# Delta mixer in 128-token tiles, its head pairs run between the input blocks; RWKV matrices alternating between heads

## The reference

```python
def mixer_c(h, w_in, conv_w, A_log, dt_bias, norm_w, w_out):
    z = h @ w_in
    qkv = jax.nn.silu(causal_dwconv(z[..., :3 * W], conv_w))
    ...
    q = l2norm(qkv[..., :W].reshape(b, s, DN_HEADS, DN_HEAD_DIM)) * (DN_HEAD_DIM ** -0.5)
    k = l2norm(qkv[..., W:2 * W].reshape(b, s, DN_HEADS, DN_HEAD_DIM))
    o = gated_delta_rule_chunked(q, k, v, g, beta)
    o = rmsnorm(o, norm_w) * jax.nn.silu(gate.astype(F32))
    return o.reshape(b, s, W).astype(h.dtype) @ w_out
```

```python
    def step(state, inp):
        v_new = u_c - jnp.einsum('bhck,bhkv->bhcv', w_c, state)
        o = jnp.einsum('bhck,bhkv->bhcv', qd_c, state) + jnp.einsum('bhij,bhjv->bhiv', at_c, v_new)
        state = state * cd_c[..., None, None] + jnp.einsum('bhck,bhcv->bhkv', kd_c, v_new)
        return state, o
```

## Time and profile before

| what | value |
|---|---|
| median of the runs | 2514.31 us |
| profiled execution | 2503.3 us, of which the span of instructions is 2501.5 us |
| TensorE matmul busy | 2377.8 us (95%) |
| VectorE, ScalarE, GpSimd busy | 1236.1, 802.5, 253.2 us |
| mean granted TensorE clock | 0.94 of full speed |
| mixer C, from its first to its last matmul | 1564.9 to 2124.5 us |

### The profile page before, as it was taken

The page is one execution under the profiler, slowest core; times in us unless marked ns, Lnnn a source line. Parts: engine busy times, 40 slices in busy tenths (PEclk is TensorE's granted clock), DMA queues, the critical chain, the costliest instruction groups (busy, mean ns, idle before and its releaser), DMA issues.

```text
span 2501.5 us, 29427 instructions
## 1 busy us (share of the span) xinstructions
PE 2377.8 (95%) x11460; PEld 1957.0 (78%) x11460; DVE 1236.1 (49%) x1528; ACT 802.5 (32%) x1053; POOL 253.2 (10%) x180
## 2 busy tenths in 40 slices
PE   6999999979988999999999999999888988999997
PEld 5888887748975888888888888877777876888886
DVE  5444445586524644443444443885665117544423
ACT  4232223452213433222323222356423124323221
POOL 1000010005500100001000011000453001000011
PEclk9999999989956999999999999999989558999999
DMA  4333323200010233332223332321000001333331
GB/s 144 98 95 99 113 83 97 76 1 1 1 35 26 93 100 92 104 104 94 85 93 100 102 104 80 96 90 51 1 1 35 1 17 59 93 96 97 111 97 52
DMA packets 48256, 182.40 MB, mean 73 GB/s; under 512 B 6320, under 2 KB 6576, under 8 KB 48176
## 3 DMA queue, kind: packets, MB, share of 16 engines
q1 hardware_dynamic: 48176, 181.29, 23.0%
HBM read 179.17 MB, written 2.10 MB: 72 GB/s over the span
## 4 chain that ended last, share of the span: by engine, by line
PE 73%; DVE 4%; ACT 2%; issue 1%; DVEq 0%; ACTq 0%
PE bank L437 18%; PE bank L439 18%; PE bank L438 18%; PE bank L500 3%; PE bank L511 3%; PE bank L822 1%; PE bank L821 1%; PE bank L607 1%; PE bank L842 1%; PE bank L833 1%; PE bank L636 1%; PE bank L851 1%; PE bank L641 1%; PE bank L514 1%; PE bank L763 1%
## 5 line engine op out<-in xcount | busy, mean ns | idle before, releaser
L437 PE MATMUL bank<-H,WS 128*128 128x512 f32 x1840 | 726.8, 395 | 26.8 <-DVE WS L1262 16.9
L438 PE MATMUL bank<-H,WS 128*128 128x512 f32 x1840 | 718.5, 390 | 0.0
L439 PE MATMUL bank<-H,WS 128*128 128x512 f32 x1840 | 718.2, 390 | 0.0
L878 ACT ACTIVATE WS<-RAW 128x1024 fp32r<-128x1024 f32 (+1 forms) x310 | 349.0, 1126 | 1082.0 <-PE bank L439 1061.0
L1262 DVE TENSOR_TENSOR WS<-RAW,WS 128x1024 fp32r<-128x1024 f32 (+1 forms) x310 | 404.6, 1306 | 252.1 <-ACT WS L878 252.0
L437 PEld LDWEIGHTS bank<-H,WS 128*128 128x128 f32 x1840 | 346.8, 188 | 108.8 <-DVE WS L1262 14.4
L438 PEld LDWEIGHTS bank<-H,WS 128*128 128x128 f32 x1840 | 346.9, 189 | 75.2 <-issue 3.8
L439 PEld LDWEIGHTS bank<-H,WS 128*128 128x128 f32 x1840 | 347.0, 189 | 72.4
L437 PE MATMUL bank<-A,WS 128*128 128x512 f32 x704 | 273.9, 389 | 0.0
L438 PE MATMUL bank<-A,WS 128*128 128x512 f32 x704 | 273.9, 389 | 0.0
L439 PE MATMUL bank<-A,WS 128*128 128x512 f32 x704 | 273.9, 389 | 0.0
(11 more groups left out here) (306 smaller groups left out, 2330.0 us busy)
## 6 DMA issues: line engine op xcount, KB each, us to landing
RAW<-in_w_gate SPq DMA_DIRECT2D x88, 512.0 KB, 3.5
RAW<-in_w_up SPq DMA_DIRECT2D x88, 512.0 KB, 3.5
RAW<-in_w_down SPq DMA_DIRECT2D x64, 704.0 KB, 4.0
RAW<-in_c_in SPq DMA_DIRECT2D x32, 512.0 KB, 3.6
RAW<-in_ab_in SPq DMA_DIRECT2D x22, 512.0 KB, 3.6
RAW<-in_ab_out SPq DMA_DIRECT2D x8, 512.0 KB, 4.4
RAW<-in_c_out SPq DMA_DIRECT2D x8, 512.0 KB, 4.1
X<-in_x SPq DMA_DIRECT2D x4, 512.0 KB, 7.2
```

The source lines that it names most:

```text
L437: pe.matmul(bank[:, :], WS[:, 0, s, cols], src[0][:, r, :], start=first and j == 0, stop=False)
L438: pe.matmul(bank[:, :], WS[:, 0, s, cols], src[1][:, r, :], start=False, stop=False)
L439: mm = pe.matmul(bank[:, :], WS[:, 1, s, cols], src[0][:, r, :], start=False, stop=last and j == len(rows) - 1)
L878: act.activation(WS[:, 0, c % SPLIT, 0:cols], RAW[:, c % RING, 0:cols], ACT.Copy).then_inc(hi_ready, 1)
```

## The change

Three things are changed.

**Mixer C works in tiles of 128 tokens.** The inverse is built for 128 tokens: after the five levels (blocks of 32, then 64) two more small products per tile join the two halves (`c_u21_mm`, `c_xt64_mm`). The solve gives u and w side by side (256 columns). The transitions are then computed in advance: for each tile a 128 x 128 matrix MT (decay times identity minus w-transposed times decayed keys) and an addition N, so that the scan is only state := MT x state + N, two steps per head (the first state is zero, the last is not needed). The outputs are one product per tile with the tile's own values plus one with the state (3 of 4 tiles). L2 norms are not applied to keys and queries; they enter as per-token factors, summed by matmuls with one column.

**Head pairs run between input blocks.** The input blocks come in the order key, query, value of a pair of heads, pair after pair, then the gates (`C_ORDER`). A unit is cut into 4 slots of 6 matmuls (`slot`). 8 units run alone; then each pair's `core(p)` runs with 24 slots between its steps. VectorE and ScalarE do the convolution, activation and splitting of a unit in `piece()`, called at the matching places. SiLU is now x(1 + tanh(x/2))/2, the first convolution tap is made by ScalarE. GpSimd multiplies token factors into RHS and KDT (6 more instructions per pair) beside the 12 masked TM. The output projection starts with the rows of heads 0 to 5.

**RWKV matrices alternate.** `matrices(b)` issues head 2b and head 2b + 1 in turn, and VectorE masks them in that order.

The core of the diff (semaphore names, allocations and the small scalar steps are left out):

```diff
+    mats += [s <= t, np.where(s <= t, 0.0, -30000.0)]
...
-                                mm = pe.matmul(BANK[4 * s + k][:, c], left[rows, b, c], right[rows, b, c],
-                                               start=True, stop=True)
-                            mm.then_inc(mat_mm[s], 1)
+                                for s in range(2):
+                                    rows = slice(s * CHUNK, (s + 1) * CHUNK)
+                                    mm = pe.matmul(BANK[4 * s + k][:, c], left[rows, b, c], right[rows, b, c],
+                                                   start=True, stop=True)
+                                    if j == TT - 1:
+                                        mm.then_inc(mat_mm[s], 1)
...
+                    def slot():
+                        t, k = divmod(next(dense), 4)
+                        if k == 0 and t >= 2:
+                            pe.wait_ge(*c_z(t - 1))
+                        unit(BANK[t % 2], u0 + t, 0, H_PARTS, (2 * k, 2 * k + 1), k == 0, k == 3, norm=n if t == 0 else None,
...
+                        for s in range(2):
+                            b0, b1, b2 = banks(s)
+                            pe.wait_ge(*c_tt(2 * p + s + 1))
+                            pe.wait_ge(*c_silu(6 * p + 2 + s + 1))
+                            for c in cols:
+                                mm = pe.matmul(b1[:, c], K[s][:, c], QQ[s][:, c], start=True, stop=True)
+                            mm.then_inc(c_qk_mm.sem, 1)
+                        slot()
...
+                        slot()
+                        if p:
+                            heads_back(p - 1)
+                        for s in range(2):
+                            b0, b1, b2 = banks(s)
...
+                        for l in range(5):
+                            for s in range(2):
...
+                                for j, c in enumerate(cols):
+                                    mm = pe.matmul(b0[:, c], CS[s]["TM"][:, j, :], CS[s]["XX"][:, j, :], start=True, stop=True)
+                                mm.then_inc(c_u_mm.sem, 1)
+                            slot()
+                            for s in range(2):
+                                b0, b1, b2 = banks(s)
+                                pe.wait_ge(*c_iu(10 * p + 2 * l + s + 1))
...
+                                for j, c in enumerate(cols):
+                                    mm = pe.matmul(b2[:, c], CS[s]["XT"][:, j, :], CS[s]["IU"][:, j, :], start=True, stop=True)
+                                mm.then_inc(c_xx_mm.sem, 1)
...
+                            slot()
...
+                        for s in range(2):
+                            b0, b1, b2 = banks(s)
+                            pe.wait_ge(*c_u21(2 * p + s + 1))
+                            pe.wait_ge(*c_xt32(2 * p + s + 1))
+                            for j, c in enumerate(halves):
+                                mm = pe.matmul(b2[lo, c], CS[s]["U21"][hi, j, :], CS[s]["XT"][hi, j, hi], start=True, stop=True)
+                            mm.then_inc(c_xt64_mm.sem, 1)
...
+                        for s in range(2):
...
+                            for j in range(TT):
+                                if j == 2 and p < 3:
+                                    pe.wait_ge(*c_kn(p + 2))
+                                mm = pe.matmul((b0, b1)[j // 2][:, j % 2 * 2 * P:(j % 2 + 1) * 2 * P], CS[s]["XT"][:, j, :],
+                                               CS[s]["RHS"][:, j, :], start=True, stop=True)
+                                if j % 2:
+                                    mm.then_inc(c_solve_mm.sem, 1)
+                        slot()
...
+                            w = CS[s]["UW"][:, :, P:2 * P]
+                            for j in (1, 2):
+                                mm = pe.matmul(b2[:, cols[j - 1]], w[:, j, :], CS[s]["KDT"][:, j, :], start=True, stop=True)
+                            mm.then_inc(c_mt_mm.sem, 1)
+                            for j in range(3):
+                                mm = pe.matmul(b0[:, cols[j]], CS[s]["KDT"][:, j, :], CS[s]["UW"][:, j, 0:P], start=True, stop=True)
+                            mm.then_inc(c_n_mm.sem, 1)
+                            for j in (1, 2, 3):
+                                mm = pe.matmul(b1[:, cols[j - 1]], w[:, j, :], CS[s]["ATT"][:, j, :], start=True, stop=True)
+                            mm.then_inc(c_qw_mm.sem, 1)
+                        slot()
+                        for k in range(2):
+                            for s in range(2):
+                                b0, b1, b2 = banks(s)
+                                pe.wait_ge(*c_mt(2 * p + s + 1))
+                                if k == 0:
+                                    pe.wait_ge(*c_n(2 * p + s + 1))
+                                else:
+                                    pe.wait_ge(*c_state(4 * p + s + 1))
+                                pe.matmul(b2[:, cols[2 + k]], CS[s]["MT"][:, k, :], CS[s]["NS"][:, k, :],
+                                          start=True, stop=True).then_inc(c_scan_mm.sem, 1)
+                            slot()
+                        for s in range(2):
+                            b0, b1, b2 = banks(s)
+                            pe.wait_ge(*c_state(4 * p + 2 + s + 1))
+                            pe.wait_ge(*c_qw(2 * p + s + 1))
...
+                    for m in range(2):
+                        mixed_rows(m, range(6))
+                    heads_back(3)
+                    for m in range(2):
+                        mixed_rows(m, (6, 7))
+                    for m in range(2, KB):
+                        mixed_rows(m, range(KB))
...
+                                act.wait_ge(*(c_ktr_mm, c_out_mm, c_vtr_mm)[kind](2 * (p - 2) + s + 1))
+                            act.activation(c_place(t)[:, :], PAD[:, t % 2, 3:3 + SEQ], ACT.Copy,
+                                           scale=par("dn_conv_w", 72 + C_ORDER[t])).then_inc(c_tap.sem, 1)
+                        u = t - 1
+                        if k == 2 and 0 <= u < C_BLOCKS:
+                            act.wait_ge(*(c_conv if u < 24 else c_z)(u + 1))
+                            if u:
+                                act.wait_ge(*c_silu(u))
...
+                            for s in range(2):
+                                h = 2 * p + s
+                                if l == 1:
+                                    pool.wait_ge(*c_ktok(2 * p + s + 1))
+                                    pool.wait_ge(*c_decays(1))
+                                    pool.tensor_tensor(CS[s]["RHS"][:, :, P:2 * P], CS[s]["KDT"][:, :, :], token_cols(EG[:, :, h]),
+                                                       ALU.mult).then_inc(c_ke.sem, 1)
...
+                                pool.wait_ge(*c_u_mm(10 * p + 2 * (l - 1) + s + 1))
+                                pool.tensor_tensor(CS[s]["TM"][:, :, :], CS[s]["TT"][:, :, :], tiles(con(f"pair{2 << l}")),
+                                                   ALU.mult).then_inc(c_tm.sem, 1)
                 squares(norm_of[phase] + 1)
...
+                        for k, (name, mask) in enumerate((("TT", "strict"), ("TKM", "strict"), ("MKM", "upper"))):
+                            for s in range(2):
+                                dst = {"TT": INV[s]["TT"], "TKM": TKM[s], "MKM": MKM[s]}[name]
...
+                        if k == 0 and 0 <= t < C_BLOCKS:
+                            vec.wait_ge(unit_done, u0 + t + 1)
+                            vec.tensor_tensor(pad[:, 3:3 + SEQ] if t < 24 else GATE_C[:, t % 4, :], BANK[t % 2][:, :], RSTD[:, :],
+                                              ALU.mult).then_inc(c_z.sem, 1)
...
+                        if k == 1 and 1 <= t < C_BLOCKS:
+                            split_lo(u0 + t + 2, 0)
+                        if k == 2 and dst is not None:
+                            vec.wait_ge(*c_z(t + 1))
+                            vec.wait_ge(*c_tap(t + 1))
+                            for r in (2, 1):
+                                step.wait()
+                                step.inc(vec.scalar_tensor_tensor(dst[:, :], pad[:, r:r + SEQ], par("dn_conv_w", 24 * r + C_ORDER[t]),
+                                                                  dst[:, :], ALU.mult, ALU.add))
+                        if k == 2 and 0 <= t - 26 < 6:
...
+                                                     ALU.mult, ALU.add).then_inc(c_conv.sem, 1)
+                        u = t - 1
+                        if k == 3 and 0 <= u < C_BLOCKS:
+                            x_ = KQV[u // 6 % 2][u % 6 // 2][u % 2][:, :] if u < 24 else GATE_C[:, u % 4, :]
+                            vec.wait_ge(*c_tanh(u + 1))
+                            vec.scalar_tensor_tensor(x_, TANH[:, :], 1.0, x_, ALU.add, ALU.mult).then_inc(c_silu.sem, 1)
...
+                        vec.wait_ge(*c_rn(p + 1))
+                        for s in range(2):
```

(27 more changed lines are left out.)

934 lines of the change are left out of this document (542 added, 392 removed).

## The result

| | before | after |
| --- | --- | --- |
| median of the runs | 2514.3 us (4 runs, 2514.1 to 2514.8) | 2382.2 us (4 runs, 2381.7 to 2383.0) |
| span of the profiled execution, mean clock | 2501.5 us, 0.940 | 2379.9 us, 0.968 |
| up to the first matmul of mixer C | 1564.9 us | 1558.2 us |
| mixer C, first matmul to the first of the next layer | 559.6 us | 444.6 us |
| from there to the end | 377.0 us | 377.1 us |

Ratio 0.9475, 95% interval 0.9458 to 0.9491. In later comparisons the executions of the kernel before fell into two groups, 2502 to 2506 us and 2514 to 2516 us; the four runs above were all in the upper one, its profiled execution in the lower. Span against span the change is worth 121.6 us: 115.0 in C and 6.6 ahead of it. The profiled execution's own time after was 2381.7.

A forecast was written before the change was run, and what follows sets the result against it. TensorE, busy 95% of the span, was taken as the bound. C's work 410.7 plus waits 48.5 gave 459.2 instead of 559.6 (100.4 less); with AB's 8.8, 2514.3 - 109.2 = 2405 us, range 2358 to 2445.

The forecast's parts named there:

- TensorE's work in C: Mixer C: four pairs' products 180.0 us, 40 units 218.4, plus tail columns, layer norm, small ones and first norms: 410.7 us.
- Clock 1.00 throughout: Mixer C: full clock assumed, because dense slots stand between products of the kind that run at 1.00 alone.
- rival C: Pairs of mixer C: small products and waits bring 1.2 GHz; 2595 us at 60% half clock; chance of slower than before 0.03.
- Decay matrix: Mixer C's pairs: attention products wait for TT, made by VectorE and ScalarE; 2.5 us per pair, 10 us.
- outputs back: Mixer C: transposes back wait for the previous pair's scaled outputs, late on VectorE; 4 us in three pairs, 12 us.
- first units: Mixer C's first 8 units: VectorE needs 5.0 of each 5.46 us, plus small dependent steps with table loads; 3 us wait.
- end: Mixer C after the last pair: some 16 us of dependent steps beside 8.2 of TensorE work; 5.5 us with one split wait.
- VectorE and GpSimd: Mixer C's levels: VectorE instructions with both operands in SBUF wait out GpSimd's, delaying IU; 4.5 us per pair, 18 us.
- Mixer AB: Alternating heads: a pair's matrices near 3.5 us, inversion 8.9 us behind their start; 2.2 us less per pair, 8.8 us.
- rival A: Mixer C: TensorE hardly waits because GpSimd and VectorE run ahead within a pair; 2365 us, chance 0.26.
- B: Mixer C's pairs: VectorE becomes the bound, 98 us per pair instead of 89; 2441 us, chance 0.22.
- D: Mixer AB: alternating heads does nothing, or products still run one by one; 2414 us, chance included in the forecast's 0.46.

The follow-up runs named there:

- Experiment 10: Kernel before, with 156 useless 128 x 128 x 128 float32 products put between the small products of mixer C's scan: 2507.3 us, ratio 0.9997.
- experiments 7 and 8: GpSimd's factors cut to 4 columns after the first pair, OTOK on ScalarE: 2373.7 us; changed kernel with the factors on ScalarE: 2375.8 us.

## Why the prediction was right, and where it was off

- **TensorE's work in C.** Forecast 410.7 us. Measured: 444.6 less 23.3 of waits less some 11 at half clock (0.03 x 340 + 0.04 x 48.6 = 12.1 by the windows, a part of it idle) gives 410. The sum of products by their pace came out within a microsecond, in part by luck, since misses of some us cancel. Two terms were too large, by about 6 us together: the 64 x 64 products with their switches (9.4 instead of 13.6 us: 0.13 us each at full clock instead of 0.16, 0.1 per switch into them instead of 0.2 per switch either way), and single-column norms (0.21 to 0.24 us instead of 0.25). Against them a slot took 1.38 instead of 1.37 (2 us in all), a transpose term was 1 us too small, and some 2 us are not assigned. The prediction had the price of a switch from the earlier trace rows, an idle 0.33 us; that row is one of the weight loads, beside which the matmuls went on. The same idle stands at each switch into the 64 x 64 products of the changed kernel, and the first of them starts 0.33 us behind the last dense matmul, where 0.23 is usual:

```profile
1764.73 0.40 PE L508 MATMUL bank<-H,WS 128*128 128x512 f32 x1
1765.06 1.14 PE L944 MATMUL bank<-c_XT,c_U 64*64 64x64 f32 x16
1765.06 1.00 PEld L944 LDWEIGHTS bank<-c_XT,c_U 64*64 64x64 f32 x16 [0.36 <-issue]
```

The Trainium skill (TensorEngine Tiling (Array Packing), Key Properties) says that a change of tiling mode drains TensorE. The idle weight loads agree with it; the price here was about 0.1 us.
- **Clock 1.00 throughout.** Nearly: 0.97 in the pairs. Experiment 10 shows that the old 0.58 came with the small products and goes when large ones stand between them. What I left out is what follows an idle stretch: in C there were six stretches of 3 to 6 us at 0.50, four behind waits of 2.6 to 4.2 us and two behind single-column norms and 64 x 64 products with hardly any idle. They cost the 11 us, and the latter two are rival C's mechanism in small.
- **Waits.** Forecast 48.5, measured 23.3. Decay matrix 10 against 4.0, outputs back 12 against 10.3, first units 3 against 0.4, end 5.5 against 4.0. The mis-sized term is "VectorE and GpSimd", 18 us: in the levels TensorE waited for IU not once but for the 4.2 us at the first pair's first level, which come from that pair's opening. The mechanism (an instruction with two SBUF operands waits out GpSimd's) is real, and experiments 7 and 8 price GpSimd's factors at 6.4 to 8.5 us (3.6 and 7.2 by the traces of C). But it acts where VectorE has no slack; in the levels it had some (busy 25.1 of the 30.0 us from 1726 to 1756, second pair). The Trainium skill's rule on the shared port (SBUF — State Buffer, SBUF: two separate sides) agrees with these rows (1.78 against 0.77, 3.44 against 1.28); it says who waits, not whether anybody waits for the one that does.
- **A pair.** Forecast 86 to 90, measured 85.3. Of the distance, the levels' 4.5 us were not there, and 1.6 us or more of half clock were.
- **Mixer AB.** The alternation works (3.7 against 3.5 us forecast), and the inversion starts 8.55 us behind (8.9 forecast). The new wait of 0.89 us for both heads' last copy, in front of each next pair's matrices, I had missed: with it a pair of AB takes 29.8 instead of 31.3 us, and the sum is 6.6 instead of 8.8.
- **The sum.** C 115.0 against 100.4, AB 6.6 against 8.8: span against span 121.6 against 109.2. C's 14.6 are about 25 us of waits forecast that were not there, less 11 at half clock that were not forecast.
- **The step from the profile to the median.** I carried the 11 us between before's profiled execution and its median over to the changed kernel. That failed: they were the distance of two groups of executions, and after has its profiled execution (2381.7) at its median. Without this step the forecast would have been 2394, 12 us above the measurement; with it, 2405, 23 above. The measured time is inside the range given, but in what rival A had for its own, although its mechanism holds only in part.
- **Rivals.** A (TensorE hardly waits) was near in the levels and wrong in the openings. B (VectorE's bound) is right for 25 us of a pair, wrong for the other 60; the 58 us of VectorE per pair that both worked with held (58.05 busy in the second pair). C's mechanism cost a few us. D is out.

What stays open: what decides whether an execution of before falls into the lower or the upper group. Of the 132 us between the medians, 121.6 are what the traces show, and the changed kernel against the lower group's 2503.5 gives 121.3; the other 11 are the group that the first runs of before fell into.

## What to carry to other kernels

Price a redesign by counting products and multiplying by their pace in the trace: that part came out within 1 us of 411, with errors of up to 6 us that cancelled. Compare span with span before a distance between a profile and a median is carried over to another kernel. A wait at a tile can be the lateness of the whole engine that makes it; before moving the tile, list what stands in that engine's queue ahead of it, and what the next tile in line would wait. And where the granted clock is low though TensorE is never idle, look at the shapes: added work in large products cost nothing at all there.

## What the runs showed of the hardware

- The scan of 64-wide float32 products ran at 1.2 GHz while busy all the time; 156 extra 128 x 128 x 128 products between them brought 2.4 GHz and left the stretch as long as it was (127 us, 129 before).
- In the changed kernel's mixer C, behind waits of TensorE of 4.2 us (three times) and 2.6 us (once) the clock fell to 0.50 for 3 to 6 us although TensorE was full again; behind one of 2.0 us it did not. Two more such stretches stood behind single-column and 64 x 64 products with hardly any wait.
- Two VectorE instructions with both operands in SBUF took 3.44 us together beside GpSimd and 1.28 without it, and removing GpSimd's instructions brought IU's wait from 4.2 to 0.9 us.
- Products of two heads from different 64-partition halves, given in turn, took 3.7 us where one head after the other took 7.00.
- At a switch from dense matmuls to 64 x 64 products the weight loads idled 0.36 us and the first product came 0.1 us later than usual.
- The same kernel's executions lay in two groups some 12 us apart. The same stretch of 24 us had a granted clock of 1.00 in one execution and of 0.51 in another with the same code up to there, which then was 11.6 us behind.
